# A decoder block on one core: the first loads in quarters, the second weight tiles ahead of the far rows, GpSimd's first sums and low parts moved forward

## What is computed

```
proj = h @ w_in[l]            # h = x, 1024 x 1024; w_in 1024 x 5840
(g_q, g_k, g_v, g_r, g_og, m_cq, m_ckv, m_kr, gate_a, gate_b) = jnp.split(proj, offsets, axis=-1)
```

## Time and profile before

| | us |
|---|---|
| median of 3 runs | 1763.31 |
| lowest and highest run | 1761.69 and 1765.01 |
| the profiled execution, its own time | 1768.03 |
| span of the profiled execution | 1766.3 |
| PE busy in it | 1732.2 (98%) |
| POOL busy | 846.8 (48%) |
| first matmul of a product starts at | 13.97 |

### The profile page before, as it was taken

One profiled execution on the slowest core, in us unless ns is written; L12 is line 12 of the kernel. 1 busy time (PEld: TensorE's weight loads), 2 busy tenths in 40 slices (PEclk: granted clock), 3 DMA queues, 4 the chain that ended last, 5 costly groups with the idle time before them and its releaser, 6 DMA issues.

```text
span 1766.3 us, 23560 instructions
## 1 busy us (share of the span) xinstructions
PE 1732.2 (98%) x8432; PEld 1452.6 (82%) x8432; DVE 1035.1 (59%) x1772; ACT 769.3 (44%) x1432; POOL 846.8 (48%) x714
## 2 busy tenths in 40 slices
PE   8999999999999999999999999999999999999998
...
GB/s 168 142 107 110 124 107 119 71 215 59 100 125 92 83 265 251 149 96 70 132 132 102 167 190 72 167 140 123 114 121 159 149 145 95 181 334 189 96 96 119
DMA packets 234110, 241.78 MB, mean 137 GB/s; under 512 B 39196, under 2 KB 162252, under 8 KB 233996
## 3 DMA queue, kind: packets, MB, share of 16 engines
...
q10 hardware_dynamic: 37920, 68.43, 11.6%
...
## 4 chain that ended last, share of the span: by engine, by line
PE 83%; DVE 7%; DMA 4%; ACT 2%; issue 2%; POOL 2%; SPq 1%; ACTq 0%; DVEq 0%; POOLq 0%
PE psum_all L1231 23%; PE psum_all L1233 23%; PE psum_all L1232 23%; PE psum_all L1563 2%; DMA ga_st<-d_sga 1%; PE psum_all L1579 1%; PE psum_all L1581 1%; PE psum_all L1580 1%; PE psum_all L1293 1%; PE psum_all L1551 1%; PE psum_all L1549 1%; PE psum_all L1550 1%; PE psum_all L1552 1%; PE psum_all L1297 1%; PE psum_all L1548 1%
## 5 line engine op out<-in xcount | busy, mean ns | idle before, releaser
L1109 POOL CAST w_hi<-w_raw 128x512 fp32r<-128x512 f32 (+3 forms) x78 | 58.3, 748 | 259.4 <-PE psum_all L1233 254.7
L1231 PE MATMUL psum_all<-xT_hi,w_hi 128*128 128x512 f32 x376 | 148.9, 396 | 5.6 <-POOL w_lo L1040 3.1
L1233 PE MATMUL psum_all<-xT_hi,w_lo 128*128 128x512 f32 x376 | 147.0, 391 | 0.0
L1232 PE MATMUL psum_all<-xT_lo,w_hi 128*128 128x512 f32 x376 | 146.9, 391 | 0.0
L1878 DVE TENSOR_TENSOR xp<-psum_all,xp 128x512 f32<-128x512 f32 x18 | 12.4, 690 | 216.6 <-PE psum_all L1233 216.6
L1231 PE MATMUL psum_all<-t_hi,w_hi 128*128 128x512 f32 x352 | 137.4, 390 | 1.2 <-DVE r L2322 0.4
L1233 PE MATMUL psum_all<-t_hi,w_lo 128*128 128x512 f32 x352 | 137.0, 389 | 0.0
L1232 PE MATMUL psum_all<-t_lo,w_hi 128*128 128x512 f32 x352 | 137.0, 389 | 0.0
L1171 POOL TENSOR_TENSOR w_lo<-w_raw,w_hi 128x512 fp32r<-128x512 f32 x88 | 115.2, 1316 | 42.1 <-ACT w_hi L3120 41.9
L1111 POOL TENSOR_TENSOR w_lo<-w_raw,w_hi 128x512 fp32r<-128x512 f32 (+3 forms) x78 | 126.7, 1624 | 6.4
L1125 POOL TENSOR_SCALAR p_sb<-p_sb,small 128x128 f32<-128x128 f32 (+3 forms) x64 | 47.8, 747 | 163.4 <-DVE small L2177 163.4
...
## 6 DMA issues: line engine op xcount, KB each, us to landing
...
```

The source lines that it names most:

```text
L1109: wc.done(nc.gpsimd.tensor_copy(w_hi[b][:, w], src[:, w]))
L1231: pe.matmul(out_ap, ah, bh, start=start and i == 0, stop=False, skip_group_check=more)
L1232: pe.matmul(out_ap, ah, bl, start=False, stop=False, skip_group_check=more)
L1233: last = pe.matmul(out_ap, al, bh, start=False, stop=stop and i == len(terms) - 1, skip_group_check=more)
```

## The change

It concerns the first 60 us or so.

- The near rows of x are loaded by column halves: four transfers of 256 KB for columns 0 to 511, later two of 512 KB for columns 512 to 1023. The two first weight tiles are loaded by contraction halves (256 KB each, on ga_in and upg_in). The order on SP is: near rows left, A11 weights, near rows right, A12 weights, second weight tiles, far rows (two transfers of 1 MB).
- PE transposes the near rows in two lots of 16. `x_first(u)` is a new form of the A11 product: high by high and low by high per k as the parts of x come, the four matmuls with the low weight part at its end. The order is A11 of u = 0, the other near transposes, A11 of u = 1, half of A12 of u = 0 (k 0, 1), two far groups, the other half, six far groups, A12 of u = 1.
- The near half of x goes to banks 1, 5, 2, 6, 3, 7 (X_BANK), so banks 0 and 4 are free for A11.
- ACT casts the weight parts of g 0 after the first near bank, g 4 and 5 before the far part of x, g 6 in its middle and g 7 behind it.
- POOL takes the sums S1 and the low parts of S1's operand ahead of the sums S2 and S4, and each S4 low part behind its sum, ahead of S3.
- ga_in gets one count more, so one later wait on it stands 16 higher.

```diff
-        X_BANK = (0, 4, 1, 5, 2, 6, 3, 7)
+        X_BANK = (1, 5, 2, 6, 3, 7, 1, 5)
...
             for t in range(4):
-                x_rows(t)
+                x_block(slice(t, t + 1), 0, tile_in[t])
             for u in range(2):
-                x_load(0, u, 0)
-            for t in range(4, TT):
-                x_rows(t)
+                x_load_first(u, 0)
+            for i in range(2):
+                x_block(slice(2 * i, 2 * i + 2), 1, tile_in[4 + i])
+            for u in range(2):
+                x_load_first(u, 1)
             for u in range(2):
                 x_load(0, u, 1)
+            for i in range(2):
+                x_block(slice(4 + 2 * i, 6 + 2 * i), None, tile_in[6 + i])
...
-            for g in range(4):
+            for g in range(2):
                 x_low(g)
             for u in range(2):
                 x_s1(0, u)
+            for g in range(2, 6):
+                x_low(g)
             for u in range(2):
                 x_s24(0, u)
-            for u in range(2):
-                x_low(x_place(0, "S1", u))
+                x_low(x_place(0, "S4", u))
             for u in range(2):
                 x_s3(0, u)
-            for g in range(6, 14):
+            for g in range(8, 14):
                 x_low(g)
...
+            x_first(0)
+            for i in range(2):
+                pe.wait_ge(tile_in[4 + i], 16)
+            x_near_t(4)
+            x_near_t(5)
+            for i in range(2):
+                pe.wait_ge(*xa("raw", i))
+                x_near_t(6 + i)
+            x_first(1)
+            pe.wait_ge(sm["snap"], 1)
+            pe.wait_ge(*xd("lo", 7))
+            x_product(0, "A12", 0, (0, 1))
+            for i in range(2):
+                pe.wait_ge(tile_in[6 + i], 16)
...
             x_snap1(0, 1)
+            x_high(4)
+            x_high(5)
             x_r12(0)
...
-            x_high(4)
-            x_high(5)
+            x_high(6)
             x_r12(2)
...
-            for g in range(6, 10):
+            for g in range(7, 10):
                 x_high(g)
```

More of the change, by code:

```diff
@@ L125, in block_kernel @@
         blk = (P, QK, HALF)
-        x_tok = [put(f"x_tok{t}", (P, D), 32 + 4 * t) for t in range(TT)]
+        x_all = put("x_all", (P, TT, D), 32)
+        x_tok = [x_all[:, t, :] for t in range(TT)]
         x1_hi, x1_lo, x2_hi, x2_lo, x3_hi, x3_lo, x4_hi, x4_lo = [
@@ L805, in parameters, with x_block, x_load_first @@
                         sp.dma_start(lat_g[:, QKT:], mla_kv_norm_g[0].rearrange("(j p) -> p j", p=P)).then_inc(par_landed, 16)
-            def x_rows(t):
-                sp.dma_start(x_tok[t][:, :], x[0, t * P:(t + 1) * P, :]).then_inc(tile_in[t], 16)
+            def x_block(ts, half, landed):
+                cs = slice(0, D) if half is None else slice(half * HALF, (half + 1) * HALF)
+                rows = x[0, ts.start * P:ts.stop * P, cs].rearrange("(t p) c -> p t c", p=P)
+                sp.dma_start(x_all[:, ts, cs], rows).then_inc(landed, 16)
+            def x_load_first(u, part):
+                ks = slice(part * QK, (part + 1) * QK)
+                at = w_raw[u][:, part * HALF:(part + 1) * HALF].rearrange("p (k c) -> p k c", k=QK)
+                sp.dma_start(at, win[:, ks, XTILES[2 * u]:XTILES[2 * u] + P]).then_inc((upg_in if part else ga_in)[u], 16)
             for t in range(4):
-                x_rows(t)
+                x_block(slice(t, t + 1), 0, tile_in[t])
             for u in range(2):
-                x_load(0, u, 0)
-            for t in range(4, TT):
-                x_rows(t)
+                x_load_first(u, 0)
[3 more added lines that the diff above has]
+                x_load_first(u, 1)
             for u in range(2):
                 x_load(0, u, 1)
+            for i in range(2):
+                x_block(slice(4 + 2 * i, 6 + 2 * i), None, tile_in[6 + i])
             for m in range(XPAIRS):
@@ L1302, in _ @@
                 pe.wait_ge(tile_in[t], 16)
-                for k in range(KT):
+                for k in range(QK):
                     last = pe.transpose(psum[X_BANK[k]][:, t * P:(t + 1) * P], x_tok[t][:, k * P:(k + 1) * P], ident[:, :])
@@ L1306, in _, with x_near_t @@
                         last.then_inc(xt_done, 1)
+            def x_near_t(k):
+                for t in range(4):
+                    last = pe.transpose(psum[X_BANK[k]][:, t * P:(t + 1) * P], x_tok[t][:, k * P:(k + 1) * P], ident[:, :])
+                last.then_inc(xt_done, 1)
             def x_rows_t(k, bk):
@@ L1323, in x_product, with x_first @@
                     last.then_inc(sm["up_mm"], 1)
-            pe.wait_ge(*xd("lo", 3))
-            for u in range(2):
-                pe.wait_ge(*xa("raw", u))
-                x_product(0, "A11", u)
-            pe.wait_ge(*xd("raw", 3))
-            for t in range(4, TT):
-                pe.wait_ge(tile_in[t], 16)
+            def x_first(u):
+                wh, wl = x_ring(u), x_ring(u, True)
+                pe.wait_ge(sm["up_hi"], u + 1)
+                for j in range(QK):
+                    near_hi, near_lo = x_moving("A11", j)
+                    js = slice(j * P, (j + 1) * P)
+                    pe.wait_ge(*xa("hi", j))
+                    pe.matmul(up_bank(u, 0), wh[:, js], near_hi, start=j == 0, stop=False)
+                    pe.wait_ge(*xd("lo", j))
+                    pe.matmul(up_bank(u, 0), wh[:, js], near_lo, start=False, stop=False)
+                pe.wait_ge(sm["up_w"], u + 1)
+                for j in range(QK):
+                    last = pe.matmul(up_bank(u, 0), wl[:, j * P:(j + 1) * P], x_moving("A11", j)[0], start=False, stop=j == QK - 1)
+                last.then_inc(sm["up_mm"], 1)
+            x_first(0)
[12 more added lines that the diff above has]
+                pe.wait_ge(tile_in[6 + i], 16)
+            pe.wait_ge(*xa("raw", 5))
+            pe.wait_ge(*xd("raw", 7))
             x_rows_t(0, 1)
             x_rows_t(1, 5)
-            pe.wait_ge(*xa("raw", 5))
-            pe.wait_ge(*xd("raw", 7))
+            x_product(0, "A12", 0, (2, 3))
             x_rows_t(4, 2)
@@ L1339, in _ @@
             x_rows_t(7, 7)
-            pe.wait_ge(sm["snap"], 1)
-            x_product(0, "A12", 0, (0, 1))
             pe.wait_ge(*xd("t1_lo", 0))
             x_rows_t(2, 1)
-            x_product(0, "A12", 0, (2, 3))
             pe.wait_ge(*xd("t1_lo", 1))
@@ L2609, in x_high @@
                 if k in (0, 1):
-                    ac.wait_ge(upg_in[u], 16 * (m + 1))
+                    ac.wait_ge(*((upg_in[u], 16 * (m + 1)) if m or k else (ga_in[u], 16)))
                 elif k == 6:
@@ L2684, in x_evict @@
                 ac.dma_start(dst[tile % 8 * P:(tile % 8 + 1) * P, half * HALF:(half + 1) * HALF], x_st[n % 2][:, :]).then_inc(sig_st[n % 2], 16)
-            for k in range(4):
+            x_near(0)
+            x_high(0)
+            for k in range(1, 4):
                 x_near(k)
-            x_high(0)
+            x_high(1)
             x_copy(0)
             x_copy(1)
-            x_high(1)
             for k in range(4, KT):
```

2 lines of the change are left out of this document (1 added, 1 removed).

## The result

The changed kernel takes 1768.22 us in the median of 20 runs (1765.09 to 1771.86), the kernel before 1765.43 in 20 runs (1761.69 to 1769.64). The ratio is 1.0013, 95 % interval 1.0007 to 1.0019: slower by 0.07 to 0.19 %. That is less than the 0.2 % that the prediction took for what can be told from no change, but with 20 runs of each the interval lies clear of it. The forecast was 1764.6 with a range up to 1767.4, so the time lies outside it.

What follows compares the result with a forecast made beforehand. PE was taken as the bound, with helper engines close behind. A 1.4 us lead at S1 became lags of 0.6 at S4 and 1.2 at S3, plus 0.1: +1.3 on 1763.31 gave 1764.6 us, range 1761.9 to 1767.4.

Steps and rivals of the forecast that it cites:

- the price of the loads: Start of the load queue: narrower x rows taken to cost 0, with bounds of 0 and 1.2 us.
- small transfers slow the queue: Rival on the eight 256 KB loads: over 1.05 us each rather than 0.78, +3.8 to 1767.1; chance 0.06.
- PE's first product near 7.7: Sign at the start of PE: A11 of u = 0 begins at 7.7 us instead of 13.97.
- PE idle for the far rows: Sign on PE before the far transposes: it waits from 19.2 until the far rows land at 20.7 us.
- the ceiling: At the far rows: PE's lead there, 0.3 + 1.4 = 1.7 us, is the most the whole change can win.
- POOL's row of work: POOL between S1 and S3 sums: 10 instructions instead of 6, S3 sums end at 34.0, 1.65 us later.
- The snapshot ahead of S4: ACT's snapshot after S1 ends at 36.25; PE stands 2.0 us, turning the 1.4 lead into a 0.6 lag.
- S3 for DVE: PE before S3: idle some 0.6 us for DVE's low part of t2, start at 42.35, lag 1.2 us.
- Behind it: After S3, near 64 us, where PE waits for ACT's snapshot: 0 to 0.3 us more lag, 0.1 taken.
- The clock falls before the far transposes: Rival on PE's idle times before 20.7 us: clock drops, +2.8 us, so 1766.1; chance 0.22.
- The lead stays: Rival behind S1: S3 sums don't hold the t3 casts, PE keeps S1's 1.4 us, so 1761.9; chance 0.12.
- The sum: Whole kernel: +1.3 us of lag, after which every engine's list is as before, giving 1764.6 us.

Runs made afterwards that it cites:

- the two profiles with pairs: Changed kernel with GpSimd's earlier order and near-left quarters as two 512 KB transfers, without or with ScalarE's casts reordered: 1761.96 and 1763.78 us.
- the second profile: The changed kernel profiled and timed once more with no edit: 1767.59 us in 11 runs, ratio 1.0009 to the kernel before.
- the far rows first: Changed kernel with the two far transfers issued ahead of the second weight tiles: 1772.12 us in a single run.
- the old list: Changed kernel with GpSimd's order behind the two S1 sums put back as in the kernel before: 1762.25 us in 12 runs, ratio 0.9991.
- ScalarE's list: Changed kernel with ScalarE's first two t3 casts and the snapshot ahead of the casts of g 8 and 9: 1765.88 us in a single run.
- the column halves: Kernel before with each of its four near row tiles loaded as two 256 KB column halves in 2 KB rows: 1765.32 us in a single run.
- both lists with pairs: Changed kernel with GpSimd's earlier order, ScalarE's casts reordered and near-left quarters as two 512 KB transfers: 1763.78 us, ratio 0.9989.

## Why the prediction was wrong

**The step that failed is the price of the loads**, "a narrower row is not priced by the trace of x; bounds: as now (0), or ... 1.2 us. I take 0", and with it "small transfers slow the queue", which had a chance of 0.06. The far rows were put at 20.7 and landed at 22.5, the second tiles at 13.4 and 15.1 and landed at 15.7 and 17.4. The change stands 1.8 us above the value taken and 0.6 above the upper bound. Nearly the whole of it is there with the first megabyte: the four near-left quarters were put at 3.4, 4.1, 4.8 and 5.5 and landed at 3.9, 4.6, 6.5 and 7.2, so the fourth was 1.7 late. In the two profiles with pairs the same megabyte landed at 6.2. What holds a quarter up is not shown; the runs say that halving the pieces costs time at the head of the stream, and how much. The rate of a filled queue, from which the 0 came, does hold, but only behind the first 2.1 MB. The earlier trace rows had a hint: the first near tiles came at 1.5 us each and the far ones at 1.3.

The Trainium skill (DMA: Bandwidth & Descriptors, Measured) asks for transfers of 1 MiB; from its figures the prediction had estimated 2.5 us more, and the runs show 0.7 from halving the transfers of 2.1 MB at equal rows (9.6 to 10.3), 1.0 to 1.6 together with the halved rows. The rule's direction holds here at the head of a stream.

Point by point:
- *PE's first product near 7.7*: 9.09, so 1.4 late, and without effect: PE waits for the far rows later anyway, as the prediction said.
- *PE idle for the far rows*: 0.79 us, at 22.59 instead of 20.7. The distance from there to S1 was forecast as 8.05 (20.7 to 28.75) and measured as 7.99 in the change and 8.00 in the six other profiles of the table with quarters or pairs and the far rows last. The wait ahead of it, for A12's low part, was forecast as 1.8 and measured as 1.19. So the ceiling and the working behind it were right, and S1 moved from a lead of 1.4 to a lag of 0.44, by 1.8.
- *POOL's row of work*: S3 sums end at 35.8, forecast 34.0, so 1.8 late, as the far rows are: POOL waits for two casts that stand on ACT behind the far part of x. The six against ten instructions and the two waits for ACT's casts (1.00 and 0.73) are as worked out.
- *The snapshot ahead of S4*: the lag was to grow by 1.4 + 0.6 = 2.0 us there; it grew by 1.87, of which 1.70 are idle time. *S3 for DVE*: 0.6 forecast, 0.60 measured, with an idle time of 0.30. *Behind it*: 0.1 forecast, 0.21 measured. So the round loses 2.7 behind S1, and 1.3 + 1.4 = 2.7 were forecast. Undoing either list removes it: the mechanism is shown.
- *The clock falls before the far transposes* (0.22): it did not. TensorE had 1.2 GHz at first (8 transposes in 1.94 us) and 2.4 GHz from 14.3 us (16 in 1.91) to 427 us, and in the second profile from 12.4 us to the last microseconds of the span. Idle times of 0.55 to 1.19 us, and one of 2.39 in the second profile, did not bring it down; the one of 7.21 with the far rows first did. The low stretch of before at 13.7 to 17.1 is gone too.
- *The lead stays* (0.12): with the old list nothing is lost behind S1 (0.06), but the lead itself had gone with the loads.
- *The sum*: 1.3 + 1.8 = 3.1 us of lag, which is what the trace shows. On the forecast's base of 1763.31 this is 1766.4, inside the range; on before's median of 20 runs it is 1768.5, against 1768.22 measured. The lower base is the other half of the miss: three runs of 1761.69 to 1765.01 fixed a median that turned out at 1765.43, and the widening by 1.7 was too little. Of the 3.6 us between 1764.6 and 1768.22 the loads are 1.8 and the base 2.1; the 0.3 too many are within the scatter.

## What to carry to other kernels

When a load is cut in pieces to let the first engine start early, price the pieces by the head of the stream and not by the rate of the filled queue, and ask what the last byte gates: here PE started 4.9 us earlier and S1 waited for the last byte. When an instruction is moved ahead in one engine's list, count what now stands between the events that others wait for, and look on the other engine for a cast in front of a snapshot; a wait with a late partner can be taken out at either end. Before a lag of zero is called slack, look whether the two sides of a balance make it.

## What the runs showed besides

**A low clock in some executions only.** At 420 to 430 us PE has 2.4 us of idle time at the end of the stage, in each kernel, and behind it TensorE got 1.2 GHz for 6.8 us in six of the 14 profiles (both of before and the change among them), for 3.4 us in five (ScalarE's list is one), and not at all in three: the second profile of the change, the old GpSimd list and the column halves. The change (us, PE, PEld, DVE, ACT, POOL, PEclk, DMA share, GB/s):

```profile
427.00:430.00 3.00, 3.00 (x15) 2.66 (x13) 0.48 (x1) 1.35 (x4) 0.00 (x0) 0.55 0.00 0
430.00:434.00 4.00, 4.00 (x20) 3.88 (x20) 1.45 (x4) 2.61 (x3) 0.00 (x0) 0.50 0.00 0
```

And its second profile:

```profile
427.00:430.00 3.00, 3.00 (x23) 2.68 (x22) 0.65 (x2) 1.52 (x5) 0.00 (x0) 1.00 0.00 0
430.00:434.00 4.00, 4.00 (x34) 3.94 (x33) 2.10 (x6) 2.44 (x3) 0.00 (x0) 1.00 0.00 0
```

Against before's profile, which has the stretch, the lag of this second profile falls from 3.70 to 0.58 behind it: the stretch costs 3.1 us, as much as the whole effect of the change up to 400 us. The runs of the old-list kernel fall in two groups, seven at 1761.6 to 1762.4 and five at 1765.0 to 1767.1; the profiled one, without the low stretch, is in the lower. The mean granted clock that the record has for each run divides them the same way: 0.998 or 0.999 in the seven, 0.996 or 0.997 in the five. Over before's 35 runs it goes from 0.999 in the fastest (1761.29) to 0.993 in the slowest (1769.60). A mean doesn't say where the low stretches lie, but 0.002 of 1762 us is 3.5 us, what a stretch of 7 us at half the clock takes (estimate), so most of the spread of one kernel goes with the clock. It may also be why medians of 12 runs scatter by 1 to 2 us around what the lags say (both lists with pairs has the smallest lag and not the smallest time), so only the lags were used for shares of a microsecond. Whether the order of the first 40 us changes how often the low stretch comes was not tried.

**A stage change at 660 to 680 us** cost PE idle times of 2.57, 0.46, 0.68 and 0.85 us in before's first profile, where its second and both of the change showed two, of 1.5 to 1.6 and 0.4 to 0.5. Over this stretch the lag of the change falls from 3.05 to -0.06, and with it the two spans of 1766.3 and 1765.9 come out the wrong way round.
